# The sums, roots and casts of a two-block kernel's norms, turned from rows to columns

## The reference, cut to what matters

```python
def rmsnorm(x, g):                       # first block; _rms in the second
    xf = x.astype(jnp.float32)
    y = xf * lax.rsqrt(jnp.mean(xf * xf, axis=-1, keepdims=True) + RMS_EPS)
    return (y * g.astype(jnp.float32)).astype(x.dtype)

def l2norm(x):                           # queries and keys of the delta net, heads of 128
    return x * lax.rsqrt(jnp.sum(x * x, axis=-1, keepdims=True) + 1e-6)

# first block, layer l
x = x + rmsnorm(mix, g_mix_post[l])      # mix: three mixers' outputs @ w_out
h = rmsnorm(x, g_ffn_pre[l])
x = x + rmsnorm(conv_geglu_ffn(h, ...), g_ffn_post[l])
# second block, layer l: x = x + gate * part(norm_mod(x)), three times
```

## Time and profile before

| | us |
|---|---|
| median of 3 runs (lowest, highest) | 3784.11 (3781.92, 3784.44) |
| the profiled execution | 3782.52 |
| its span, first to last instruction | 3780.8 |
| TensorE busy, matmuls | 3608.8 |
| VectorE busy | 2171.2 |
| ScalarE busy | 1203.7 |
| GpSimd busy | 362.2 |

### The profile page before, as it was taken

The page is one execution under the profiler, slowest core; times in us unless marked ns, Lnnn a source line. Parts: engine busy times, 40 slices in busy tenths (PEclk is TensorE's granted clock), DMA queues, the critical chain, the costliest instruction groups (busy, mean ns, idle before and its releaser), DMA issues.

```text
span 3780.8 us, 52186 instructions
## 1 busy us (share of the span) xinstructions
PE 3608.8 (95%) x19222; PEld 2906.2 (77%) x19222; DVE 2171.2 (57%) x3513; ACT 1203.7 (32%) x1787; POOL 362.2 (10%) x545
## 2 busy tenths in 40 slices
PE   8989899999989899989999998999999999999999
PEld 6768688877768688878887766888778877667887
DVE  5867588645877678545544655555343336554332
ACT  3344333323334333222222344222222223442221
POOL 1101011100201011101110101111000001010000
PEclk9999999999999999999999999999999999999999
DMA  4300255532300255425543302455333332113333
GB/s 111 83 23 3 60 158 159 143 91 74 82 13 17 72 160 162 134 84 156 161 143 104 80 24 61 138 162 146 106 89 100 87 103 70 34 45 89 96 88 95
DMA packets 580059, 359.84 MB, mean 95 GB/s; under 512 B 20414, under 2 KB 559792, under 8 KB 579888
## 3 DMA queue, kind: packets, MB, share of 16 engines
q1 hardware_dynamic: 554480, 281.43, 27.0%
q0 software_dynamic: 25408, 76.11, 6.7%
HBM read 355.35 MB, written 2.10 MB: 95 GB/s over the span
## 4 chain that ended last, share of the span: by engine, by line
PE 80%; DVE 11%; issue 3%; DMA 2%; ACT 2%; DVEq 1%; POOL 0%; ACTq 0%; SPq 0%; POOLq 0%
PE ps L1431 17%; PE ps L1433 16%; PE ps L1432 16%; PE ps L1680 6%; PE ps L1684 6%; PE ps L1683 6%; DMA wada<-in_w_ada 2%; DVE wl L2253 1%; PE ps L1596 1%; PE ps L1576 1%; PE ps L1865 1%; PE ps L1554 1%; DVEq L2256 1%; PE ps L1529 1%; PE ps L1643 1%
## 5 line engine op out<-in xcount | busy, mean ns | idle before, releaser
L1431 PE MATMUL ps<-hh,wh 128*128 128x512 f32 x3168 | 1261.1, 398 | 54.2 <-DVE wl L2253 22.8
L1433 PE MATMUL ps<-hh,wl 128*128 128x512 f32 x3168 | 1242.8, 392 | 0.0
L1432 PE MATMUL ps<-hl,wh 128*128 128x512 f32 x2912 | 1142.3, 392 | 0.0
L2253 DVE TENSOR_TENSOR wl<-wring,wh 128x1024 fp32r<-128x1024 f32 x500 | 611.4, 1223 | 779.6 <-ACT wh L841 771.8
L841 ACT ACTIVATE wh<-wring 128x1024 fp32r<-128x1024 f32 x528 | 556.6, 1056 | 1032.3 <-PE ps L1433 524.6
L1431 PEld LDWEIGHTS ps<-hh,wh 128*128 128x128 f32 x3168 | 600.2, 189 | 209.0 <-issue 49.7
L1433 PEld LDWEIGHTS ps<-hh,wl 128*128 128x128 f32 x3168 | 599.8, 189 | 128.0
L1432 PEld LDWEIGHTS ps<-hl,wh 128*128 128x128 f32 x2912 | 552.7, 190 | 112.6 <-issue 1.9
L1680 PE MATMUL ps<-ah,wh 128*128 128x512 f32 x1056 | 411.9, 390 | 2.0 <-DVE wl L2253 2.0
L1684 PE MATMUL ps<-ah,wl 128*128 128x512 f32 x1056 | 410.9, 389 | 0.0
L1683 PE MATMUL ps<-al,wh 128*128 128x512 f32 x1056 | 410.9, 389 | 0.0
(11 more groups left out here) (421 smaller groups left out, 3390.3 us busy)
## 6 DMA issues: line engine op xcount, KB each, us to landing
wring<-in_w_ffn_up SPq DMA_DIRECT2D x176, 512.0 KB, 4.9
wada<-in_w_ada POOLq DMA_DIRECT2D x384, 192.0 KB, 2.7
wring<-in_w_in SPq DMA_DIRECT2D x98, 512.0 KB, 5.1
wring<-in_ffn_w_up SPq DMA_DIRECT2D x88, 512.0 KB, 4.9
wring<-in_w_ffn_down SPq DMA_DIRECT2D x64, 512.0 KB, 3.9
wring<-in_w_out SPq DMA_DIRECT2D x32, 512.0 KB, 5.0
wring<-in_ffn_w_down SPq DMA_DIRECT2D x32, 512.0 KB, 3.9
wring<-in_w_ffn_down SPq DMA_DIRECT2D x16, 384.0 KB, 3.5
```

What stands on the lines that cost most here:

```text
L1431: pe.matmul(dst, w, h, start=first, stop=False)
L1432: pe.matmul(dst, w, hlo, start=False, stop=False)
L1433: return pe.matmul(dst, wlo, h, start=False, stop=last)
L2253: v.tensor_tensor(wl[:, w, :, :], wring[:, p, h, :, :], wh[:, w, :, :].bitcast(F32), ALU.subtract)\
```

## The change

All these sums get their tokens on the partitions. The square of a token group becomes the stationary operand (128 x 128) and one column of ones the moving one, so that a sum is one column of 128 numbers; a wide norm has 4 columns, the row norms of heads 16 or 32. Root and reciprocal then work on 128 x 4, 128 x 16 or 128 x 32. For the cast the broadcast column of `rstd` is the stationary operand and the identity the moving one. In the norms that accumulate over squares, a matmul of the identity with 4 columns of the stair that are zero opens the bank first (two passes more). The second block's head norms that call `row_sums` and `row_cast` with bank 4 stay as they are. `column_part` takes the place of `stair_part`, `column_roots` that of `row_roots`, and `wide_cast` serves the first norm too.

```diff
-                s.activation(std[0:NT, 0:P], ps[0:NT, 7, 0:P], ACT.Sqrt, bias=epsc[0:NT, 0:1], scale=1.0 / D)\
+                s.activation(std[:, 0:NT], ps[:, 7, 0:NT], ACT.Sqrt, bias=epsc[:, 0:1], scale=1.0 / D)\
...
-                s.activation(std[0:32, 0:P], ps[0:32, 7, 0:P], ACT.Sqrt, bias=epsc[0:32, 0:1])\
+                s.activation(std[:, 0:8 * NT], ps[:, 7, 0:8 * NT], ACT.Sqrt, bias=epsc[:, 0:1])\
...
-                deviation(4 * NT, P, P)
+                deviation(P, 4 * NT, P)
...
-            def stair_part(m, n):
-
-                R = NT * n
+            def column_part(m):
+
                 sq_ready.next(pe)
                 if m == 0 and n_norm[0]:
                     pe.wait_ge(std_done.sem, n_norm[0])
                 for t in range(NT):
                     j = NT * m + t
-                    i = pe.matmul(ps[0:R, 7, 0:P], stair[:, 31 - j:31 - j + R],
-                                  sq[:, n_sq[0] % 4, t * P:(t + 1) * P], start=j == 0, stop=j == R - 1)
+                    i = pe.matmul(ps[:, 7, j:j + 1], sq[:, n_sq[0] % 4, t * P:(t + 1) * P], ones[:, 0:1],
+                                  start=True, stop=True)
...
-                        i = pe.matmul(ps[:, 1 + m % 3, t * P:(t + 1) * P], ident[:, j:j + 1].broadcast_to([P, P]),
-                                      rstd[:, 0:P], start=True, stop=True)
+                        i = pe.matmul(ps[:, 1 + m % 3, t * P:(t + 1) * P], rstd[:, j:j + 1].broadcast_to([P, P]),
+                                      ident[:], start=True, stop=True)
...
+                pe.matmul(ps[:, b, 0:NT], ident[:], stair[:, 0:NT], start=True, stop=False)
                 for j, slot in enumerate((0, sum_slot(KD - 1))):
                     if j:
                         sq_ready.next(pe, KD)
                     for t in range(NT):
-                        m = pe.matmul(ps[0:NT, b, 0:P], stair[:, 31 - t:31 - t + NT], sq[:, slot, t * P:(t + 1) * P],
-                                      start=j == 0 and t == 0, stop=j == 1 and t == NT - 1)
+                        m = pe.matmul(ps[:, b, t:t + 1], sq[:, slot, t * P:(t + 1) * P], ones[:, 0:1],
+                                      start=False, stop=j == 1 and t == NT - 1)
...
             def wide_norm():
 
-                row_sums(7, KD)
-                row_cast(6)
+                for k in range(KD):
+                    sq_ready.next(pe)
+                    if k == 0:
+                        if n_norm[0]:
+                            pe.wait_ge(std_done.sem, n_norm[0])
+                        pe.matmul(ps[:, 7, 0:NT], ident[:], stair[:, 0:NT], start=True, stop=False)
+                    for t in range(NT):
+                        m = pe.matmul(ps[:, 7, t:t + 1], sq[:, n_sq[0] % 4, t * P:(t + 1) * P], ones[:, 0:1],
+                                      start=False, stop=k == KD - 1 and t == NT - 1)
+                    m.then_inc(sq_used.sem, 1)
+                    n_sq[0] += 1
+                wide_cast()
+
+            def wide_cast():
+
+                nr_done.next(pe)
+                for n in range(NT):
+                    m = pe.matmul(ps[:, 6, n * P:(n + 1) * P], rstd[:, n:n + 1].broadcast_to([P, P]), ident[:],
+                                  start=True, stop=True)
+                m.then_inc(nr_cast.sem, 1)
...
-                v.reciprocal(rstd[0:NT * n, 0:P], std[0:NT * n, 0:P]).then_inc(rec_done.sem, 1)
+                v.reciprocal(rstd[:, 0:NT * n], std[:, 0:NT * n]).then_inc(rec_done.sem, 1)
...
-                if columns:
-                    v.reciprocal(rstd[:, 0:NT], std[:, NT:2 * NT]).then_inc(nr_done.sem, 1)
-                else:
-                    v.reciprocal(rstd[0:NT, 0:P], std[0:NT, 0:P]).then_inc(nr_done.sem, 1)
+                at_ = NT if first else 0
+                v.reciprocal(rstd[:, 0:NT], std[:, at_:at_ + NT]).then_inc(nr_done.sem, 1)
```

More of the change, by code:

```diff
@@ L1517, in row_norms @@
                 for m in range(n):
-                    stair_part(m, n)
+                    column_part(m)
                 n_norm[0] += 1
-            def stair_part(m, n):
-                R = NT * n
+            def column_part(m):
                 sq_ready.next(pe)
@@ L1776, in _ @@
                             pe.wait_ge(ix_relu.sem, 12)
-                        stair_part(n - 9, 8)
+                        column_part(n - 9)
                 n_norm[0] += 1
@@ L1797, in beside @@
                             j = NT * m + t
-                            x = pe.matmul(ps[:, BESIDE, t * P:(t + 1) * P], ident[:, j:j + 1].broadcast_to([P, P]),
-                                          rstd[:, 0:P], start=True, stop=True)
+                            x = pe.matmul(ps[:, BESIDE, t * P:(t + 1) * P], rstd[:, j:j + 1].broadcast_to([P, P]),
+                                          ident[:], start=True, stop=True)
                         x.then_inc(bc_done.sem, 1)
@@ L2010, in _ @@
                 for h in HEADS:
-                    stair_part(h, 4)
+                    column_part(h)
                 n_norm[0] += 1
@@ L2020, in _ @@
                         j = NT * h + t
-                        i = pe.matmul(ps[:, FACTORS[h], t * P:(t + 1) * P], ident[:, j:j + 1].broadcast_to([P, P]),
-                                      rstd[:, 0:P], start=True, stop=True)
+                        i = pe.matmul(ps[:, FACTORS[h], t * P:(t + 1) * P], rstd[:, j:j + 1].broadcast_to([P, P]),
+                                      ident[:], start=True, stop=True)
                     i.then_inc(bc_done.sem, 1)
@@ L2272, in root, with column_roots @@
                 rec_done.next(v)
-            def row_roots(n):
+            def column_roots(n):
                 std_done.next(v)
-                v.reciprocal(rstd[0:NT * n, 0:P], std[0:NT * n, 0:P]).then_inc(rec_done.sem, 1)
+                v.reciprocal(rstd[:, 0:NT * n], std[:, 0:NT * n]).then_inc(rec_done.sem, 1)
                 rec_done.next(v)
@@ L2292, in sum_add, with wide_root @@
                     n_sq[0] += KD
-            def wide_root(splits=0, columns=False):
+            def wide_root(splits=0, first=False):
                 v.drain()
                 nr_std.next(v)
-                if columns:
-                    v.reciprocal(rstd[:, 0:NT], std[:, NT:2 * NT]).then_inc(nr_done.sem, 1)
-                else:
-                    v.reciprocal(rstd[0:NT, 0:P], std[0:NT, 0:P]).then_inc(nr_done.sem, 1)
+                at_ = NT if first else 0
+                v.reciprocal(rstd[:, 0:NT], std[:, at_:at_ + NT]).then_inc(nr_done.sem, 1)
                 for n in range(splits):
@@ L2304, in wide_root, with pre_norm @@
                 nr_cast.next(v)
-            def pre_norm(g, shift=None, splits=0, columns=False):
-                wide_root(splits, columns)
+            def pre_norm(g, shift=None, splits=0, first=False):
+                wide_root(splits, first)
                 def low(k):
@@ L2568, in _ @@
                 else:
-                    pre_norm(block_1_gain, splits=2, columns=True)
+                    pre_norm(block_1_gain, splits=2, first=True)
                     v.wait_ge(const_ready.sem, 2)
@@ L2666, in _ @@
                 pick(4)
-                row_roots(8)
+                column_roots(8)
                 pick(4)
@@ L2901, in _ @@
                         i.then_inc(hg_s.sem, 1)
-                row_roots(4)
+                column_roots(4)
                 def normed(h):
```

## The result

| | us |
|---|---|
| before, median of 5 runs (lowest, highest) | 3782.47 (3780.74, 3784.44) |
| changed, median of 5 runs (lowest, highest) | 3802.31 (3797.54, 3804.74) |
| ratio, 95% interval | 1.0047, 1.0036 to 1.0058 |
| span of the profiled execution, before and after | 3780.8, 3800.7 |

The account below looks back on a forecast made before the run. TensorE, busy 95% of the span, bounds the kernel; -8.1 - 4.5 + 19.2 + 3.6 + 3.2 + 3.6 = +17.0 on 3782.5 gives 3799.5 us. Own range 3789 to 3811; 8 in 10: 3781 to 3812.

Parts of the forecast that it names:

- (a): Roots and reciprocals of the 13 wide norms: shorter, net 0.75 us at eight norms, 0.7 at three, nothing at two; -8.1 us.
- (e): Casts of the other norms: clock sometimes fallen when they start, half of 0.9 us at seven; +3.2, bounds 0 and +6.4.
- (b): Sixteen sets of sums between products: 1.36 us instead of 1.64 each; -4.5 us, or nothing if VectorE became the bound.
- (c): Four wide norms with squares summed one by one: half clock throughout, 14.3 us of sums for 9.5; +19.2 us.
- (d): Casts of the four norms summed one by one, then at half clock: 2.08 us instead of 1.17; +3.6 us.
- (f): 32 passes in a row before the first mixer's output norm: clock falls, 1.8 us per layer; +3.6, bounds 0 and +7.
- (g): Casts keep their size; first products after a gap run at half clock before and afterwards: nothing, bounds -3 and +4.
- Rival 3: Slower still: low clock lasts into first products after most wide norms, 1.7 us at ten; 3816 us, chance 0.07.
- Rivals 1 and 2: Clock comes back during column sums: 1, column sums hold it, 3770 us, chance 0.13; 2, halfway through, 3781 us, chance 0.08.

## Why the prediction was right

- **(a) roots, -8.1.** Sqrt 0.264 (taken 0.27), reciprocal 0.178. The 0.10 us taken off for the wider weight load was 0.02 (eight sums 1.07 for 1.05), so a root is worth 0.85, not 0.75, where it is on the path; at the norms at 837 and 1671 us it is worth nothing, as forecast. At the five norms that stand outside the pairs the sum gave 2 x 0.75 + 3 x 0.7 = 3.6 us; the table above has 3.9, with (e) in it, which is near nothing there. In all -9.3, by what the other terms leave of the trace's difference.
- **(b) sums inside products, -4.5.** -3.5 in both traces, 15 x 0.26 less 0.5 at the set behind which GpSimd is waited for; 4.5 by the runs, with 1 to 8 possible. The sum had only VectorE in mind as what could hold TensorE up there.
- **(c) four long norms, +19.2.** 14.24, 14.21, 14.24 and 14.21 us, at half clock from first to last, where 14.3 was worked out from 66 passes at the cadence of L1811. Against 9.47, 9.27, 9.47 and 9.52 before, +19.2. That row had a load of 4 rows where these have 128; it made no difference.
- **(d) their casts, +3.6.** 2.08 us each, +3.7. Pair by pair (a), (c) and (d) give +4.2 at 459 and 1289 and +4.95 at 857 and 1691; measured +3.98, +5.21, +4.93, +4.67.
- **(e) casts of the other norms, +3.2.** In this trace two sets of casts went to half clock (at 1282 and 2091 us, +0.9 each), two that had been wholly or partly slow before became faster (1.57 to 1.36 and 2.08 to 1.45): +1.0. But the size is right over the traces: in the five other versions with these nine norms in columns and no added matmul the nine casts take 1.3, 1.9, 3.6, 3.6 and 3.6 us more than before, and in the three with these norms in rows at most 0.3 us less. So the one-column sums do cost the casts their clock, though how often differs from one execution to the next.
- **(f) the 32 passes, +3.6.** From the first pass to the first product behind, the kernel before took 9.20 us in both layers, and so did each of the seven other versions with these passes in rows. The four with one-column passes took 9.27 twice, 10.8 four times and 12.35 twice, 10.8 on average: 1.6 us per layer, +3.2. So the loss is owed to the change and near what was forecast, though it is spread unevenly; in this trace it all falls in layer 1.
- **(g)** The first products behind a gap: 38.4 us at half for 40.5, so neither gain nor loss. Rival 3 asked for 1.7 us more at each of ten.

Terms (a) to (f) as measured, with 0.3 us for the sums at 1279 that ran at half clock, come to about 19.9 - 5.4 = 14.6 in the trace, where the forecast had 17.0; the rest is clock that differs between two executions, and no term stood for it. The runs weigh it differently: the long norms alone +18.9 and the rest of the change -5.7 (interval -9.5 to -1.9), together 13, for a measured difference of 18 (14 to 22). Those two ratios and this one carry 4 to 6 us each of uncertainty, so they agree only roughly. The mechanism and its size, (c) and (d), were right; that 3799.5 came within 3 us of 3802.3 is luck, as those 5.4 us made up for terms that came out lower.

The forecast's own range, 3789 to 3811, isn't what half of the bounds gives: it is all the bounds of (e) to (g) at once, -9.8 and +10.6, and (c)'s lower bound is left to the rivals. Half of them would be 3795 to 3805, and that too holds the measured time.

Rivals 1 and 2 fell with the windows: the clock did not come back in any of the four. The trace sided against the reading of the Trainium skill ("TensorE: Matmul & The Clock Gate", Part 1) by which a busy TensorE gets its clock: here PE was busy for 14.17 to 14.19 of 14.20 us at 0.50. If "busy" on that page means columns moved, not time in which the record shows an instruction, the runs with 1, 64 and 128 columns agree with it.

## What to carry to other kernels

Turning a reduction so that its result has tokens on partitions makes the small work behind it cheap (0.85 us less per root and reciprocal here) and the reduction itself nearly nothing to TensorE's clock, which behaves as if the engine rested. So do it where other matmuls surround it (-0.26 us per set) and no other engine is waited for behind it, and keep the 128-column form where it is all that TensorE has to do for several microseconds (+4.8 us per norm). When a TensorE that is the bound has to wait for other engines just before its long stream of products, a matmul whose result nobody reads, short enough to end before the operand is ready, can be worth more than the tuning of the wait: 10 to 12 us of 3784 here, in rows or in columns. Its size was not varied. And a record of a TensorE that is busy from end to end is no sign of full clock: read the granted clock beside it. With 64 columns to a pass it stayed at half, with 128 it came back; what lies between was not run.

## What the runs showed that was not expected

The clock's answer was not gradual: 1 and 64 columns per pass give the same half clock throughout (sums 14.2 and 14.7 us), 128 give it back after 3.9 to 6.2 us. The weight loads slow down with the clock as well, as the loads of the long norms by line show (ns min/median/max), the changed kernel with 128 columns first, the changed kernel second:

```profile
L1640 PEld LDWEIGHTS ps<-ones,sq x256: 192/192/338, 446.1 to 1692.8; 128*128 128x128 f32 x128
```

```profile
L1635 PEld LDWEIGHTS ps<-ones,sq x256: 333/333/337, 440.6 to 1709.3; 128*128 128x128 f32 x128
```

And whole stretches of attention had a clock of 0.82 in one execution and 0.95 in another, worth 3 us each way. Part of this looks like more than chance. In all eight versions that have the 16 sets with their root and casts in columns, the first layer's attention takes 1.6 to 3.4 us less than in the kernel before and the second layer's 1.6 to 3.3 us more, the 32 passes taken out; in the three that have them in rows the differences are -0.7 to +0.4 and -0.2 to +1.2. The two nearly cancel (-0.7 to +0.9 together), so no term of the sum misses them, but one stretch of one trace read by itself would have been put down to the wrong thing. What in the edit moves them, the casts within the attention or only the earlier start, no run here separates.
